# Layer norm of a convolution block: variance summed one token per partition instead of broadcast to every partition

## The reference

```python
def layernorm(x, g, b):
    mu = jnp.mean(x32, axis=-1, keepdims=True)
    xc = x32 - mu
    var = jnp.mean(xc * xc, axis=-1, keepdims=True)
    y = xc * lax.rsqrt(var + EPS) * g + b

    u = lax.conv_general_dilated(u, w_dw, ...) + b_dw      # depthwise, width 31
    u = jax.nn.silu(layernorm(u, ln_g, ln_b))
    return u @ w_pw2 + b_pw2
```

## Time and profile before

| | |
|---|---|
| time, median of 3 runs | 1803.39 us (1803.2 to 1804.93) |
| the profiled execution | 1802.55 us, its span 1800.7 us |
| TensorE busy | 1747.2 us (97%) |
| VectorE busy | 1018.8 us (57%) |
| ScalarE busy | 716.1 us (40%) |
| mean granted TensorE clock | 0.992 |

### The profile page before, as it was taken

One profiled execution on the slowest core, in us unless ns is written; L12 is line 12 of the kernel. 1 busy time (PEld: TensorE's weight loads), 2 busy tenths in 40 slices (PEclk: granted clock), 3 DMA queues, 4 the chain that ended last, 5 costly groups with the idle time before them and its releaser, 6 DMA issues.

```text
span 1800.7 us, 20998 instructions
## 1 busy us (share of the span) xinstructions
PE 1747.2 (97%) x8014; PEld 1383.3 (77%) x8014; DVE 1018.8 (57%) x1268; ACT 716.1 (40%) x1064; POOL 248.9 (14%) x183
## 2 busy tenths in 40 slices
PE   7987999999999999999999999999999999999997
PEld 6874788888888777788888888756557778888886
DVE  6898654424444556654424444569856677537753
ACT  5776532312233344432212223464554454324431
POOL 0783100000001000100000004572200200000001
PEclk9998999999999999999999999999999999999998
DMA  5220322322231321222322232423202122322221
GB/s 183 71 71 10 117 95 102 118 95 73 106 118 69 121 71 53 83 99 93 128 70 94 93 128 79 150 77 111 88 24 82 59 94 102 120 70 94 102 97 47
DMA packets 28052, 164.62 MB, mean 91 GB/s; under 512 B 4511, under 2 KB 5675, under 8 KB 11596
## 3 DMA queue, kind: packets, MB, share of 16 engines
q1 hardware_dynamic: 25088, 158.11, 25.2%
q10 hardware_dynamic: 2892, 5.55, 1.0%
HBM read 156.28 MB, written 4.47 MB: 89 GB/s over the span
## 4 chain that ended last, share of the span: by engine, by line
PE 80%; DVE 10%; POOL 5%; ACT 3%; issue 2%; DMA 0%; POOLq 0%; DVEq 0%; SPq 0%; ACTq 0%
PE PS L627 25%; PE PS L629 25%; PE PS L628 25%; POOL CV L1765 4%; DVE PS L1943 2%; DVE W_lo L1893 2%; ACT W_hi L1182 1%; DVE WK L2333 1%; DVE TOP L2331 1%; DVE SSUM L2374 1%; PE PS L1067 1%; POOL ISC L1837 1%; DVE PS L2510 0%; DVE X L2513 0%; PE PS L1078 0%
## 5 line engine op out<-in xcount | busy, mean ns | idle before, releaser
L627 PE MATMUL PS<-H_hi,W_hi 128*128 128x512 f32 x1600 | 640.1, 400 | 14.7 <-DVE H_lo L1873 10.4
L629 PE MATMUL PS<-H_hi,W_lo 128*128 128x512 f32 x1600 | 624.7, 390 | 0.0
L628 PE MATMUL PS<-H_lo,W_hi 128*128 128x512 f32 x1600 | 624.2, 390 | 0.0
L1182 ACT ACTIVATE W_hi<-W_raw 128x2048 fp32r<-128x2048 f32 (+2 forms) x130 | 262.6, 2020 | 672.2 <-PE PS L629 672.2
L627 PEld LDWEIGHTS PS<-H_hi,W_hi 128*128 128x128 f32 x1600 | 301.0, 188 | 101.9 <-issue 36.6
L1893 DVE TENSOR_TENSOR W_lo<-W_raw,W_hi 128x2048 fp32r<-128x2048 f32 (+2 forms) x130 | 332.2, 2556 | 59.4 <-ACT W_hi L1182 59.1
L629 PEld LDWEIGHTS PS<-H_hi,W_lo 128*128 128x128 f32 x1600 | 300.8, 188 | 64.4
L628 PEld LDWEIGHTS PS<-H_lo,W_hi 128*128 128x128 f32 x1600 | 301.3, 188 | 59.1 <-issue 1.2
L627 PE MATMUL PS<-HID_hi,W_hi 128*128 128x512 f32 x640 | 249.5, 390 | 1.5 <-DVE HID_lo L2029 1.4
L1740 POOL TENSOR_TENSOR SSUM<-SSUM,SQ 128x512 f32<-128x512 f32 x43 | 63.6, 1479 | 1351.0 <-ACT SQ L1224 1349.5
L628 PE MATMUL PS<-HID_lo,W_hi 128*128 128x512 f32 x640 | 249.0, 389 | 0.0
(11 more groups left out here) (302 smaller groups left out, 1506.8 us busy)
## 6 DMA issues: line engine op xcount, KB each, us to landing
W_raw<-in_inp SPq DMA_DIRECT2D x13, 1024.0 KB, 4.8
W_raw<-in_pw SPq DMA_DIRECT2D x11, 1024.0 KB, 4.8
W_raw<-in_gu0a SPq DMA_DIRECT2D x11, 1024.0 KB, 4.8
W_raw<-in_gu0b SPq DMA_DIRECT2D x11, 1024.0 KB, 4.8
W_raw<-in_gu1a SPq DMA_DIRECT2D x11, 1024.0 KB, 4.8
W_raw<-in_gu1b SPq DMA_DIRECT2D x11, 1024.0 KB, 4.7
W_raw<-in_gu2a SPq DMA_DIRECT2D x11, 1024.0 KB, 4.8
W_raw<-in_gu2b SPq DMA_DIRECT2D x11, 1024.0 KB, 4.8
```

The costliest lines, as they stand in the source:

```text
L627: nc.tensor.matmul(dst[:], wh, x_hi[:, k, :], start=(k == first), stop=False)
L628: nc.tensor.matmul(dst[:], wh, x_lo[:, k, :], start=False, stop=False)
L629: return nc.tensor.matmul(dst[:], wl, x_hi[:, k, :], start=False, stop=(k == last))
L1182: nc.scalar.activation(W_hi[b][:, 0:n], W_raw[b][:, 0:n], ACT.Copy).then_inc(w_hi, 1)
```

## The change

The sum of squares of each tile becomes four products: weights are 128 tokens of squares, one column of ones streams, and the result goes to columns 0 to 3 of `PS[1]`. ACT takes the root of these four columns, DVE their reciprocal. TensorE waits for it, spreads the factors over `PS[3]` with `token_spread`, and then runs three idle products where there were seven. DVE's scaling of the tiles reads `PS[3]` where it read `T_g`.

```diff
+CONV_LN = 8
-TOKEN_NORMS = [MIX0, MIX_POST, FFN_PRE, FFN_POST]
+TOKEN_NORMS = [MIX0, CONV_LN, MIX_POST, FFN_PRE, FFN_POST]
@@ TensorE
-                nc.tensor.matmul(PS[1][:], ones, LN_SQ[m % 4], start=(n == 0), stop=(n == len(LN_SUMS) - 1)).then_inc(ln_var_ready, 1)
+                for b in range(4):
+                    last = nc.tensor.matmul(PS[1][:, b:b + 1], tokens(LN_SQ[m % 4], b), ones[:, 0:1], start=(n == 0 and b == 0),
+                                            stop=(n == len(LN_SUMS) - 1 and b == 3))
+                last.then_inc(ln_var_ready, 1)
+            pe.wait_ge(ln_r, 1)
+            token_spread(PS[3], r_ps)
             pe.wait_ge(const2_in, 16)
-            idle_products(PS[2], 7)
+            idle_products(PS[2], 3)
@@ ScalarE
-            nc.scalar.activation(STD[:], PS[1][:], ACT.Sqrt, bias=epst[:], scale=1.0 / D_MODEL).then_inc(ln_std, 1)
+            nc.scalar.activation(STD4[:], PS[1][:, 0:4], ACT.Sqrt, bias=epst[:], scale=1.0 / D_MODEL).then_inc(ln_std, 1)
@@ VectorE
-            nc.vector.reciprocal(T_g[:], STD[:]).then_inc(ln_r, 1)
-            dve.wait_ge(ln_r, 1)
+            nc.vector.reciprocal(R4[:], STD4[:]).then_inc(ln_r, 1)
+            dve.wait_ge(r_ps, TOKEN_NORMS.index(CONV_LN) + 1)
-                nc.vector.tensor_tensor(CV[:, m, :], CV[:, m, :], T_g[:], ALU.mult).then_inc(ln_scaled, 1)
+                nc.vector.tensor_tensor(CV[:, m, :], CV[:, m, :], PS[3][:], ALU.mult).then_inc(ln_scaled, 1)
```

## The result

The changed kernel takes 1806.22 us (median of 20 runs, 1804.55 to 1808.72), the kernel before 1803.43 us (20 runs beside them). The ratio is 1.0014, 95% interval 1.0007 to 1.0020: a loss of 2.8 us, 1.3 to 3.6 by the interval. I had forecast 1805.7 in a range of 1801.6 to 1808.4: a loss of 2.3 us, too small to be told from no change, and the measured one is as small.

What follows compares the result with a forecast made beforehand. TensorE was taken to bound the kernel, without slack behind the convolution's norm. Squares done later +2.8, root, reciprocal and spread -1.6, idle products beyond `pw2`'s readiness +1.1 gave +2.3 us on 1803.39: 1805.7 us, range 1801.6 to 1808.4.

Steps and rivals of the forecast that it cites:

- TensorE's next real product sets the time: Whole kernel: the chain that ended last is 80% TensorE, so only moving TensorE's next real product counts.
- There is no slack behind the norm: Behind the convolution's norm: a microsecond won or lost before `pw2` shifts the kernel's end by one.
- anything else: Remaining outcomes, such as another stretch meeting the clock at another moment; chance 0.03.
- The full-clock sum: Convolution's norm at full clock: root and reciprocal take 1.62 us in place of 4.10, a gain of 2.5 us.
- The fall of the clock: Sums of squares in the convolution's norm: clock falls to half at 173.5 to 174.4 us, taken as 174.0.
- The pace at half clock: Sums of squares after the fall: one-column records every 0.2125 us, against 0.112 at full clock.
- Rival B: Convolution's norm: clock falls but sums keep 0.112 us a record; gain 0.6 us, 1802.8 us; chance 0.12.
- The rise of the clock: Idle products before `pw2`: clock rises 2.4 to 5.3 us after the first, at 185.8 to 188.8, middle 187.3.
- idle products beyond `pw2`'s readiness: End of the convolution's norm: slow idle products run on after `pw2` is ready, costing +1.1 us.
- my case: Convolution's norm: clock falls and sums slow; loss 2.3 us, range +1.0 to +3.3, floor 1.2; chance 0.58.
- A: Convolution's norm: the clock holds because records fill the stretch; 2.5 us won, 1800.9 us; chance 0.07.
- C: Start of `pw2`: clock is still low when it runs; +4.5 us, 1807.9 us; chance 0.20.

Runs made afterwards that it cites:

- the repeat: The changed kernel run once more, unaltered, for another profile, against the kernel before: ratio 1.0012 (1.0003 to 1.0021), median 1806.29 us.

## Why the prediction was right, point by point

**TensorE's next real product sets the time.** Right up to 1150 us, and right on average between the kernels with 128 columns and three or seven idle products. "There is no slack behind the norm" left out that the stretch from 1150 to 1350 us can take up to 3.4 us more of its own, in kernels whose work is shifted and in the one with seven idle products whose work is not. The prediction had this only as its 0.03 of anything else.

**The full-clock sum.** Forecast 2.5 us won; with 128 columns, which hold the clock, 2.3. Root to spread was 0.53 in both the forecast and the profile. DVE's operand in PSUM cost nothing: four scalings in 2.48 us against 2.50 before.

**The fall of the clock.** Forecast at 3.6 to 4.4 us after the last wide record, measured 4.8 and 4.0 in the changed kernel. It was the decisive step, and it came from two other norms of the same trace. That both showed a fall was in part luck. MIX_POST had one in all three profiles of the kernel before, but with the same one-column sums it had none in five of the twelve profiles. In FFN_POST the fall met the spread in the first profile only; in the other two it came behind TensorE's last product, at 1792.16 and 1793.08. So one-column sums do not bring a fall each time; in the convolution's norm, whose sums have 56 records where MIX_POST has 24, all four profiles with 1 or 32 columns have one. Nor is the delay after the last wide product a property of the work: between the two profiles of the changed kernel it differs by 0.8 us.

**The pace at half clock.** Forecast 0.2125 us a record, from a spread. Measured: eight one-column records in 1.84 us, one lasting 0.35, so (1.84 - 0.35)/7 = 0.213. Rival B is out. The Trainium skill, "TensorE: Matmul & The Clock Gate", section "LDWEIGHTS (loading the stationary operand)", gives a load as the columns over 1.2, with no clock in it; at half clock these traces disagree. In the timeline of the changed kernel's weight loads, eight took 1.83 us at half clock, and sixteen 1.86 at full.

```profile
172.82 1.86 PEld L792 LDWEIGHTS PS<-cmat,SQ 128*128 128x128 f32 x16 [2.34 <-issue]
...
178.54 1.83 PEld L792 LDWEIGHTS PS<-cmat,T_u 128*128 128x128 f32 x8
```

**The moments.** Counted from the first subtraction: root forecast 11.2 us after it (181.2 - 169.99), measured 10.84 and 11.4 (182.20 - 171.36; 181.69 - 170.31). Scalings forecast at 13.7, measured 13.48 in the first profile. By the terms of the sum: squares done later, forecast +2.8, measured +2.4 and +3.0; root, reciprocal and spread, forecast -1.6, measured -1.5 in both.

**The rise of the clock.** Forecast 2.4 to 5.3 us after the first idle product; measured 1.8 (184.60 to 186.39) and 3.8 (184.09 to 187.91). The term for idle products beyond `pw2`'s readiness, forecast +1.1, measured 0.0 and +0.6: it was put too high. In the first profile the rise was early and the loss in the norm was 1.0, the floor of my case (1.2) less the late fall. In the second the loss was 2.1 to `pw2` and 2.45 to the later point. Forecast: 2.3.

**Rivals.** A (the clock holds) is not what the changed kernel does, and one edit makes it so; that edit gave 2.3 of the 2.5. The section "Why this matters for your kernels" of the Trainium skill's "TensorE: Matmul & The Clock Gate", which looks to idle gaps between bursts, did not describe this norm: the gaps stayed and the fall went when the columns came. It does describe the kernel before with three idle products, where the clock fell in a pause of TensorE of 4.82 us. C (half clock in `pw2`) came in small: the repeat's first product lasted 0.79 us, and of the kernels with the change only the one without idle products paid much, 1.8 us behind it.

The result is +2.8 by the medians and +2.3 by the means of all runs. The two profiles have +1.0 and +2.45 in the norm, the stretch from 1150 to 1350 us adds some 2.1 in both, and the time from 1440 us on 1.0 and 0.9. Against the mean of before the sum is smaller, since its profiled executions are quicker than its mean. How the mean over many executions divides between the norm and the rest is not settled. The forecast counted the norm alone and put the rest at nothing, so that the total came within 0.5 us of it is in part luck; the mechanism in the norm is not.

## What to carry to other kernels

Products with one streaming column followed each other no faster than those with 128 (0.112 and 0.117 us), as if the weight load, which both have, set the pace. Only the wider ones kept the clock up through the convolution's norm: 128 in all four profiles, 64 in its one. Where sums are taken with the data as weights, stream a full block of ones and read one column of it. When idle products are cut, count what TensorE does in their place: here they bought 2.2 us in one kernel, 0.8 in another, and cost 2.5 in a third, by whether the clock needed them. For an edit of a few microseconds, measure its stage from a fixed event to a fixed event; the time of the kernel carries the falls of the clock elsewhere.

## What the runs showed of the hardware that I had not expected

The clock fell after TensorE's one-column records had filled 3.29 of 3.29 us. A stretch can be full of such records and be followed by half clock.

Half clock nearly doubled the distance between one-column records behind 128x128 weights, from 0.112 to 0.213 us, though they stream next to nothing.

The falls in the convolution's sums came 160.43 us after the clock's first rise in all four profiles that have one, wherever the work stood. A repeat of one program moved the fall by 0.8 us against the work, and the norm's length by 1.15 us (16.71 and 17.86), while the kernel before, whose clock held there, repeated to within 0.02 us over 70.5.
